# Norms between dense stages: their steps are placed by what ScalarE and VectorE have been given, and a stage's first products ask only for the H chunk that they take

## What is computed

```
def first_block(x, ...):
    x = x + 0.5 * rms_norm(swiglu(rms_norm(x, ffn1_pre_g), ...), ffn1_post_g)
    y = hybrid_mixer(rms_norm(x, mix_pre_g), ...)      # attention + linear recurrence
    x = x + rms_norm(y, mix_post_g)
    x = x + 0.5 * rms_norm(swiglu(rms_norm(x, ffn2_pre_g), ...), ffn2_post_g)

def second_block(x, c, ctx, ...):                       # layers 0 (retention), 1 (neighbourhood attention)
    a = modulate(h, m[0], m[1])
    h = layer_norm(ALPHA * h + m[2] * mixer(a), ...)
    f = swiglu_2(modulate(h, m[3], m[4]), ...)
    h = layer_norm(ALPHA * h + m[5] * f, ...)
```

## Time and profile before

| | us |
|---|---|
| median of 3 runs | 2988.85 |
| lowest and highest | 2985.76, 2996.08 |
| the profiled execution | 2984.38 |
| its span, first to last instruction | 2982.8 |
| PE busy | 2869.7 |
| DVE busy | 1547.2 |
| ACT busy | 1077.0 |
| GpSimd busy | 540.2 |

### The profile page before, as it was taken

One profiled execution on the slowest core, in us unless ns is written; L12 is line 12 of the kernel. 1 busy time (PEld: TensorE's weight loads), 2 busy tenths in 40 slices (PEclk: granted clock), 3 DMA queues, 4 the chain that ended last, 5 costly groups with the idle time before them and its releaser, 6 DMA issues.

```text
span 2982.8 us, 40716 instructions
## 1 busy us (share of the span) xinstructions
PE 2869.7 (96%) x16352; PEld 2490.8 (84%) x16352; DVE 1547.2 (52%) x2691; ACT 1077.0 (36%) x1870; POOL 540.2 (18%) x288
## 2 busy tenths in 40 slices
PE   7999989899999999999999899999999999999998
PEld 7888886888878888888888788888887777888887
DVE  5666568556675653444445644444564525532224
ACT  4322247443232542332323722112235535442222
POOL 2343200023333011011110011111111212022220
PEclk9999999899999999999999899999999999999999
DMA  4544312124443111021110123322312121123221
GB/s 141 175 162 165 118 59 76 66 85 170 154 157 121 72 50 64 29 71 43 54 60 29 48 95 107 106 83 98 131 51 102 47 71 56 65 87 106 98 99 36
DMA packets 84699, 268.84 MB, mean 90 GB/s; under 512 B 8992, under 2 KB 16544, under 8 KB 84128
## 3 DMA queue, kind: packets, MB, share of 16 engines
q1 hardware_dynamic: 84512, 266.25, 26.0%
HBM read 262.54 MB, written 2.10 MB: 89 GB/s over the span
## 4 chain that ended last, share of the span: by engine, by line
PE 83%; DVE 6%; ACT 3%; issue 2%; DMA 1%; POOL 1%; SPq 0%; DVEq 0%; ACTq 0%; POOLq 0%
PE ps L1404 26%; PE ps L1405 26%; PE ps L1406 26%; PE ps L1604 1%; ACT t_whi L1660 1%; DVE t_m L2043 1%; PE ps L1631 1%; DVE t_wlo L1955 1%; PE ps L1615 1%; POOL t_wlo L2413 1%; DMA t_x<-in_ctx 1%; PE ps L1497 1%; DVE t_m L1975 0%; PE ps L1489 0%; DMA t_raw<-in_ada 0%
## 5 line engine op out<-in xcount | busy, mean ns | idle before, releaser
L1404 PE MATMUL ps<-t_h,t_whi 128*128 128x512 f32 (+1 forms) x2368 | 829.9, 350 | 28.7 <-POOL t_wlo L2413 15.9
L1405 PE MATMUL ps<-t_h,t_wlo 128*128 128x512 f32 (+1 forms) x2368 | 823.5, 348 | 0.0
L1406 PE MATMUL ps<-t_h,t_whi 128*128 128x512 f32 (+1 forms) x2368 | 822.3, 347 | 0.0
L2413 POOL TENSOR_TENSOR t_wlo<-t_raw,t_whi 128x1024 fp32r<-128x1024 f32 (+3 forms) x149 | 359.4, 2412 | 1698.2 <-ACT t_whi L1660 1698.2
L1404 PEld LDWEIGHTS ps<-t_h,t_whi 128*128 128x128 f32 x2368 | 453.0, 191 | 93.6 <-issue 22.3
L1405 PEld LDWEIGHTS ps<-t_h,t_wlo 128*128 128x128 f32 x2368 | 453.5, 191 | 55.4 <-issue 1.0
L1406 PEld LDWEIGHTS ps<-t_h,t_whi 128*128 128x128 f32 x2368 | 452.9, 191 | 55.0
L1660 ACT CAST t_whi<-t_raw 128x1024 fp32r<-128x1024 f32 (+3 forms) x327 | 326.2, 998 | 303.4 <-PE ps L1406 281.7
L1404 PE MATMUL ps<-t_hid,t_whi 128*128 128x256 f32 (+1 forms) x1306 | 425.0, 325 | 7.9 <-DVE t_hid L2088 5.6
L1405 PE MATMUL ps<-t_hid,t_wlo 128*128 128x256 f32 (+1 forms) x1306 | 422.0, 323 | 0.0
L1406 PE MATMUL ps<-t_hid,t_whi 128*128 128x256 f32 (+1 forms) x1306 | 421.3, 323 | 0.0
(11 more groups left out here) (275 smaller groups left out, 3970.2 us busy)
## 6 DMA issues: line engine op xcount, KB each, us to landing
t_raw<-in_gu SPq DMA_DIRECT2D x176, 512.0 KB, 3.2
t_raw<-in_ada SPq DMA_DIRECT2D x96, 512.0 KB, 3.2
t_raw<-in_dn SPq DMA_DIRECT2D x52, 512.0 KB, 3.5
t_raw<-in_dn SPq DMA_DIRECT2D x24, 384.0 KB, 3.2
t_raw<-in_ret_v SPq DMA_DIRECT2D x16, 512.0 KB, 3.2
t_raw<-in_ret_qk SPq DMA_DIRECT2D x16, 512.0 KB, 3.2
t_raw<-in_ret_g SPq DMA_DIRECT2D x16, 512.0 KB, 3.1
t_raw<-in_ret_o SPq DMA_DIRECT2D x16, 512.0 KB, 3.6
```

The costliest lines, as they stand in the source:

```text
L1404: e.matmul(out, whi, xlo, start=first, stop=False, skip_group_check=shared)
L1405: e.matmul(out, wlo, xhi, start=False, stop=False, skip_group_check=shared)
L1406: return e.matmul(out, whi, xhi, start=False, stop=last, skip_group_check=shared)
L2413: e.tensor_tensor(m.block(1, it.slot, n), m.raw(it), m.block(0, it.slot, n), ALU.subtract).then_inc(*S["lo_pool"].of(j))
```

## The change

No instruction is new; the order of the list is made in another way.

- A table EFFORT gives for most kinds of items the time on ACT and on DVE. `put` adds it up into `until`, the time until which each of the two has been given work, beside `now`, the sum of PE's estimated time. While the larger `until` is more than AHEAD = 1.0 beyond `now`, `tick` puts in no step of a chain.
- `need(ver, c, s)` stands ahead of each step of `by_steps` and of each chunk of `rows_by_group`: it puts in steps of half s's chain only until that chunk has been sent, and then counts on `now` up to `until`. The rest of the chain is forced only after the eight steps, or after the group's rows.
- `chain_bank(s)` first forces the chain that held the bank last, if it isn't at its end.
- The numbers that chains yield are others: 1.8 and 1.6 in place of 2.4 and 1.2 around the diagonal, 0.8 for 1.1 per chunk of an rms norm, 0.5 for 0.8 per chunk of a layer norm, and the waits before the first root_sum and after the squares of a layer norm follow `until`.

```diff
+EFFORT = {
+    "square": (0.33, 0), "sum": (0, 0.34), "mean": (0, 2.7), "gated": (0, 0.4), "na_o": (0, 0.4), "ln_apply": (0, 0.4), "ln_send": (1.0, 0.34),
...
+AHEAD = 1.0
...
     def put(kind, **kw):
         items.append(Work(kind=kind, id=len(items), **kw))
+        if kind in ("rms_send", "mod_send", "ln_send"):
+            sent.add((kw["ver"], kw["c"], kw["s"]))
+        for i, us in enumerate(EFFORT.get(kind, (0, 0))):
+            if us and not (kind == "prep_lo" and low[kw["j"]] == "lo_pool"):
+                until[i] = max(until[i], now[0]) + us * kw.get("n", 256) / 256
         return items[-1]
...
     def tick(us):
 
-        for s in sorted(chains):
+
+        now[0] += us
+        for s in chains:
             chains[s][0] -= us
-            while s in chains and chains[s][0] <= 0:
+        s = 0
+        while s is not None:
+            s = next((s for s in sorted(chains) if chains[s][0] <= 0), None)
+            if s is None or max(until) > now[0] + AHEAD:
+                break
+            chains[s][0] = max(chains[s][0], -0.5)
+            step(s)
+
+    def need(ver, c, s):
+
+        if (ver, c, s) not in sent:
+            while (ver, c, s) not in sent:
                 step(s)
+            tick(max(0, max(until) - now[0]))
...
         for si, (t0, n) in enumerate(segs):
-            force_tokens(t0, n)
+            if by_blocks or specs[0][3][0] != "h":
+                force_tokens(t0, n)
...
             for k in range(nk):
+                if src[0] == "h":
+                    for s in range(t0 // 256, (t0 + n) // 256):
+                        need(src[1], k, s)
                 put("step", groups=groups, k=k, first=k == 0, last=k == nk - 1, src=src, t0=t0, n=n)
                 tick(len(groups) * (n + 32) / 800)
                 yield
+            force_tokens(t0, n)
...
-            chains[s] = [4.5 if square and s == 1 else 1.6, chain(s)]
-
-    def chain_bank():
+            chains[s] = [max(1.6, max(until) - now[0] + 0.5), chain(s)]
+
+    def chain_bank(s):
+
         i = turn["chain"] = turn.get("chain", 0) + 1
-        return (6, 7)[i % 2]
+        b = (6, 7)[i % 2]
+        was, steps = at_bank.get(b, (None, None))
+        if was in chains and chains[was][1] is steps:
+            force(was)
+        at_bank[b] = s, chains[s][1]
+        return b
```

## The result

| | before | after |
|---|---|---|
| median, us | 2991.64 (6 runs, 2985.76 to 2996.08) | 3040.89 (6 runs, 3035.98 to 3042.22) |
| span of the profiled execution | 2982.8 | 3040.4 |

The changed kernel is slower: ratio 1.0163, 95% interval 1.0149 to 1.0176, that is 45 to 53 us. I forecast 3024 and a range up to 3042: the median lies 1.1 us inside the upper end, and one of the six executions (3042.22, the profiled one) just outside it.

The account below looks back on a forecast made before the run. TensorE, 96% busy, bounds the kernel, leaving 113 us idle plus lower-clock stretches. Terms 4.5+8+10.3-5.3+6.9+2.3+2.1+2.7 = 31.5, with the clock 40, on the profiled 2984.4 give 3024; range 2984 to 3042.

Parts of the forecast that it names:

- the mixer's scale: First norm into the mixer, second half: squares behind block 1's exponentials, next product about 10.15 after the scores' end; +7.
- Retention: Third norm into retention: context-token rows no longer force the norm; waits 0.63, 1.46, 1.25 and 1.7 of clock go; -5.3.
- Layer norm into the second attention: Entry of the second attention: PE's wait of 6.94 becomes about 8.6 and a short wait is added; +2.3.
- Its end into f4: Second attention's end into f4: 2.04 and 3.82 stay in sum, second half's sends lose two covering products; +2.1.
- count nothing: Four more table loads, 5.1 us of ACT, run while ACT waits for a root sum or PE; nothing counted.
- Clock: Half-clock stretches behind new idle at start, mixer, f2 and f3: 1.7, 3.4, 1.7, 1.7 more; +8.5, bounds 0 and 14.
- Splits: Some weight splits change between GpSimd and DVE, five rows fewer on GpSimd, 1.22 us each on DVE, beside PE's work.
- Signs: Norm-product waits 40 to about 60; 7 idle after block 1's scores; 12 before f3; f2's root sum behind cast; retention waitless.
- A: Forced steps are done early, since ACT and DVE run ahead of PE; 2986 to 2991; chance 0.13 together with D.
- B: Faster: stages start after some chunks while the rest arrives; half of it gives 2956, a third 2966; chance 0.13.
- C: Delays in the mixer run into its own waits, both norms' half clock is full; 3040 and more; chance 0.03.
- D: Holding does nothing, since estimates are never over the present by more than 1; A's time; chance 0.13 with A.

Follow-up runs that it names:

- the first run: The kernel before with the table EFFORT, its bookkeeping and the holding of chains in the tick alone: 3059.89 us, ratio 1.0234.

## Why the prediction was right, and where its steps failed

- **Sign and mechanism.** Right. The loss sits at the boundaries, in DVE and ACT queues of small steps behind casts, splits and exponentials; at the mixer's scale and at f2's cast an edit shows it, elsewhere the rows do. Forecast waits against measured: f3 12.2 and 12.05, f2's forced sums 2.0 and 1.88, start 3.4 and 3.21, steps 0 to 2 of the mixer 6.5 and 5.94. For the mixer's scale I named some 7 us of idle time; it is 7.85 and 1.07, and my own walk (10.15 less root sum and root row) had given 8.6. In f2 the new waits are 15.0 in sum, not 13.5, above all since the first send of the second half makes PE wait 4.22, not 2.5.
- **The number.** 3024 against 3040.89 is within the range, by 1.1 us. A change of 40 was forecast, the medians moved by 49.3.
- **Retention.** The size was right (-5.3 and -5.2), the reason wrong, so the hit is luck. I wrote that the rows of the context tokens stand in front of the norm and no longer force it. Written out in the kernel before, that edit alone gives the same list, item for item: the rows force only half 2. The norm moves because its chain is held, or its delays and asking act together: the entry gains 5.3 with holding alone, 4.9 with all but holding, and loses with either of the others.
- **Layer norm into the second attention, 2.3 against 8.1: the mis-sized term.** The first wait was right (8.6 forecast, 8.20 measured, 1.3 above). "A short wait is added" was 1.39 before the next half's diagonal and 1.51 before its first chunk, and I had counted no clock there: the stretches at half clock around it are 17.1 us where before had 6.8, and the 5.62 busy us of the window shown cost 2.8.
- **Its end into f4, 2.1 against 8.4: the other one.** "2.04 and 3.82 stay in sum" was wrong by 0.6 (4.19 and 2.30), and the second half's first send costs 4.65, not 2.1. ACT and DVE ahead of it:

```profile
2664.68 1.28 ACT L1772 ACT_TABLE_LOAD   x1
2665.97 0.38 ACT L1772 ACTIVATE t_m<-ps 128x256 f32<-128x256 f32 x1
...
2667.47 0.42 DVE L2133 TENSOR_TENSOR t_hid<-t_tmp,t_hid 128x256 fp32r<-128x256 f32 x1 [0.59 <-ACT t_hid L1777]
2667.82 1.26 DVE L2073 SCALAR_TENSOR_TENSOR t_m<-t_m,t_par,ps 128x256 f32<-128x256 f32 x3
```

  PE had done root_row at 2665.35; the applies start at 2667.82, because the drain of a single product stands ahead of them on DVE, and it waits for a table load that the square root between two drains has made necessary. I had seen these loads and "count nothing": that is the step that failed. Before, this stretch had two loads, 1.28 us each, now four; the six traces of kernels with all chains held have four, all others two. How much of the 4.65 the drain makes and how much the load I did not try, so the load's part is read from the rows and not shown by an edit. The Trainium skill, ScalarE: Activation LUTs, section "Table sets: the hidden batching unit", by which functions of one set should stay together, pointed at this place; the load's length was the 1.28 of the trace. The stretches at half clock at this entry are 17.1 us, where before had 6.8.
- **Clock.** 8.5 forecast, with 14 as the upper bound; 16.2 measured. By place, as half of PE's busy time inside the stretches at 0.50, it is 4.1 more at the start (forecast 1.7), 3.5 in the mixer (3.4), 4.8 in f2 (1.7), 1.7 less at retention, 1.1 less at f3 (1.7 more), 4.4 more in the second attention with its entry and 3.2 more at f4 (nothing forecast for either). So the term was right in the mixer and at retention and mis-sized at every other entry.
- **Splits.** "All beside PE's work" holds for this change in its result, but not as a rule: shifted by one they cost 5.6 us by medians. "Five rows fewer on GpSimd" was misread: it is 13 splits fewer (288 and 275 instructions on GpSimd), and 145 blocks changed engines.
- **The base.** In the start the table above flatters me. Six other traces, whose lists are before's up to there, come 0.3 to 4.9 us later than its profile at 100 us, 2.5 in the middle; six with the changed order come 4.8 to 7.3 later. So the start costs about 3 us, not 7.3, and the forecast of 6.2 was about twice too high. The profiled execution of before, 2984.38, is the quickest but one of 54 (2984.19 to 2996.08); medians lie at 2989 to 2992. From profile to profile the loss is 57.6, from median to median 49.3. I left the 4.5 us between that execution and the median out. That was a second error, of the same sign: added to the median of six, 2991.64, the 40 would have given 3031.6; the other 9 are the steps' own.
- **Signs.** Four of my five were seen: the 7 us before the root sum of the mixer's scale, 12 before f3, f2's root sum behind a cast, none at retention. The first was not: the waits before the norms' two products went down, from 40.2 to 36.2, not up to 60. I had asked for them there while my own sum had them before steps.
- **Rivals.** A fell: the queues were as late as I had walked them, with waits of 7.85, 12.05 and 8.20. B was at best true in part: against holding alone the changed kernel gives back 22.2 us at f3 and the second attention, which asking by chunk may explain, but asking alone costs some 10 us and gains nowhere. C, "more than I count", with 3040 and more and a chance of 0.03, has the time: the clock's cost is above my bound of 14, as C said, but the mixer's own wait did not grow (3.19 before, 3.23 now). D fell with the first run.

## What to carry to other kernels

Walk the order of every in-order queue at a stage's boundary, and give each wait found there its stretch at half clock and each forced square root its table load: the two terms that I sized as waits alone (2.3 and 2.1) were a quarter of what was measured (8.1 and 8.4). A scheduler's choice that depends on a count (here which engine splits a block) moves far from the edit; hold it fixed when a change is tried. And a step that holds work back until an engine is less loaded puts it behind whatever the hand-written part of the list adds meanwhile.

## What I had not expected of the hardware

- A table load was 1.28 us in each row read here, and ACT's next instruction started at its end where it had nothing else to wait for (load at 2664.68, L1772 at 2665.97).
- The same list of work runs with its stretches at half clock in other places from execution to execution. With no edit near it, one run has 20.4 us at 0.50 where another has 0.75 in the same part of the mixer; by place it costs about 4 us. The run with the cast moved, then the changed kernel:

```profile
546.20:566.60 20.40, 18.41 (x86) 18.11 (x86) 10.68 (x26) 7.22 (x14) 0.00 (x0) 0.50 0.17 53
```

```profile
546.20:566.60 20.40, 16.67 (x101) 16.37 (x102) 14.48 (x35) 8.95 (x19) 0.00 (x0) 0.75 0.16 53
```

  So a difference of under 5 us between two traces is no effect by itself: it needs the medians, or a wait that is there in one and not in the other.
